# Weighting a one-hot matrix on ScalarE instead of VectorE, in a two-block transformer kernel

## The chip, the cores and the metric

The kernel runs on one core of one Trainium2 chip. The metric is the device time of one execution in microseconds (us). An execution of the kernel before takes 3455.06 us (median of 3 runs, 3452.7 to 3456.17).

## The reference

Two transformer blocks in fp32 over 512 tokens of width 1024: a hybrid of gated delta rule and sparse attention with a gated feed-forward, then a hybrid of two linear-attention mixers with a PEER feed-forward. The change lies in that last one. PEER holds 16384 experts, numbered by pairs of 128 x 128 keys. For each token and each of 8 heads it takes the 16 best pairs with softmax weights:

```
        idx = jnp.take_along_axis(cand_idx.reshape(n, PEER_HEADS, -1), pos, axis=-1)
        w = jax.nn.softmax(best, axis=-1)
        u = jnp.take(u_tab, idx, axis=0)
        act = jax.nn.gelu(jnp.einsum('nhkd,nd->nhk', u, hb).astype(jnp.float32))
        out = jnp.einsum('nhk,nhkd->nd', w * act, jnp.take(v_tab, idx, axis=0))
```

Each token so has 128 chosen experts (i, j) with weights w.

## The kernel before

The program is written engine by engine, with its own semaphores; nothing is reordered by a scheduler. For the first 64 tokens the experts' rows are gathered by GpSimd. For the other 448 the kernel works densely, in two stages:

- **The u stage** multiplies all 16384 experts by the 448 tokens. Each fp32 product is made of three matmuls (high times high, high times low, low times high). `u_pe` has 128 steps t of two halves with 12 matmuls of 128x448 each; two steps share one weight tile of 128x2048, so a tile ends with every odd step. ScalarE (`u_sc`) makes the high part of the tile two ahead as soon as the tile before it in the same buffer is used up (`next_high`, line 516, `wh`), and then a gelu (line 2959, `gst`) after each step. VectorE (`u_ve`) makes the low part (line 523, `wl`). SyncE (`u_sy`) loads tiles (`ring<-in_u`) and spills each gelu to HBM (`gelu_spill<-gst`); there are two `gst` buffers, and a gelu waits until the spill two steps earlier has landed.
- **The v stage** reads the gelus and a dense 128x128 table of weights per token back, multiplies them (`weigh`) and multiplies the result by the v table.

The dense weight tables are built beside the u stage, from the chosen pairs. `choose` does this in four blocks j of 128 tokens: `top` finds the best 16 pairs per head (VectorE mostly), `hot` builds the tables of the block. For a token, two one-hot matrices of 128 pairs by 128 keys are formed on VectorE and multiplied on TensorE: `Bh` says the second key of each pair, `Ah` the first key and carries the pair's weight. `ijw` holds i, j and w of the block with the 128 pairs on the partitions, one column per token. A step of `hot` handles four tokens, called a quad here; there are 112 (16 in block 0, 32 in each of blocks 1 to 3). `Ah` and `Bh` have three buffers each. Per quad:

- `hot_ve`, VectorE: one comparison of 128x512 for `Bh` (line 2895) and four instructions of 128x128 for `Ah` (lines 2897 to 2899), each a comparison and a multiplication by the weight at once; then semaphore `ab`. From the fourth quad on it first waits for the products of three quads earlier (`ab_mm`).
- `hot_pe`, TensorE: waits for `ab`, then four products into one of three PSUM banks (line 2865; the matmuls themselves are issued on line 568), `ab_mm`. Each fp32 product counts as two matmuls in the trace, so a quad shows as x8.
- `hot_sc`, ScalarE: waits for `ab_mm`, then copies the bank into `stage` (line 2879), `stg`. `hot_sy` spills `stage` after every 16 quads (`weight_spill`, four transfers of SyncE).

`weave` fixes the order of each engine's instructions: the steps of the u stage and of `choose` alternate one to 1.05, and within `choose` the steps of `hot(j)` and `top(j + 1)` alternate one to 0.75, the last block's `hot(3)` running alone. `hot_ve` starts its first quad two steps before `hot_pe` does. Every engine executes its own list strictly in this order:

```
    CHOOSE = 1.05
...
        together((u_pe(p), 1), (choose_pe(p), CHOOSE))
...
            yield from weave((hot(j), 1), (top(j + 1), 0.75))
```

Of the kernel before, what the change touches and what calls it, by code (L numbers as in the profile page):

```python
# [7 lines left out]
ALU = mybir.AluOpType  # L8
ACT = mybir.ActivationFunctionType
AX = mybir.AxisListType  # L10
M, A_, S_ = ALU.mult, ALU.add, ALU.subtract
# [140 lines left out]
def bc(ap, n):  # L152
    a = ap.unsqueeze(2)
    return a.to_broadcast([a.shape[0], a.shape[1], n])


def rep(ap, n):
    a = ap.unsqueeze(1)
    return a.to_broadcast([a.shape[0], n, a.shape[2]])


def flat(ap):
    return ap.rearrange("p a b -> p (a b)")


def quad(ap):
    return ap.rearrange("p (a b) -> p a b", a=4)
# [47 lines left out]
def build(nc, D, shapes):  # L215
    with ExitStack() as ctx:
        _build(nc, D, ctx)
# [56 lines left out]
def _build(nc, D, ctx):  # L274
    s = Sems(nc, ctx)
# [3 lines left out]
    def sb(name, shape, dt=F32, c=ctx):  # L279
        return c.enter_context(nc.sbuf_tensor(name, shape, dt))  # L280

    cst = sb("cst", [128, D["consts"].shape[1]])
    C = {k: cst[:, o:o + n] for k, (o, n) in CONST.items()}
# [166 lines left out]
    with ExitStack() as ar:  # L450
# [9 lines left out]
        ijw = sb("ijw", [128, 3, 128], F32, ar)  # L460
        red8 = sb("red8", [128, 2, 8], F32, ar)
        Ah = [sb(f"Ah{j}", [128, 4, 128], F32, ar) for j in range(3)]
# [103 lines left out]
    def mm(p, out, pairs, start=True, stop=True, check=True):  # L566
        for i, (l, r) in enumerate(pairs):
            ins = p.e.matmul(out, l, r, start=start and i == 0, stop=stop and i == len(pairs) - 1,  # L568
                             skip_group_check=not check)
        return ins  # L570
# [7 lines left out]
    def tr(p, out, in_):  # L578
        k = in_.shape[0]
        return p.e.transpose(out, in_, ident[0:k, 0:k])  # L580
# [2261 lines left out]
    def quads(j):  # L2842

        return [(32 * j + q - 16, q) for q in range(16 if j == 0 else 0, 32)]
# [3 lines left out]
    def hot_pe(p, j):  # L2848
        yield
        yield  # L2850
        p.wait_ge(s("wsel"), j + 1)
        if j:
            p.wait_ge(s("ijw"), j)
        for c in range(3):
            ins = tr(p, bank[4][:, 128 * c:128 * c + 128], sel[:, c, :])
        p.then_inc(ins, s("ijw_mm"))
        yield
        yield
        yield
        for t, q in quads(j):  # L2860
            if t >= 3:
                p.wait_ge(s("stg"), t - 2)
            p.wait_ge(s("ab"), t + 1)
            for z in range(4):
                ins = mm(p, bank[5 + t % 3][:, 128 * z:128 * z + 128], [(Ah[t % 3][:, z, :], Bh[t % 3][:, z, :])],
                         start=z == 0, check=False)
            p.then_inc(ins, s("ab_mm"))
            yield
        yield

    def hot_sc(a, j):
        for _ in range(5):
            yield
        for t, q in quads(j):
            b, place = t // 16, stage[t // 16 % 2]
            if b >= 2:
                a.wait_ge(s(f"wst{b % 2}"), 64 * (b // 2))
            a.wait_ge(s("ab_mm"), t + 1)
            a.then_inc(a.e.activation(place[:, :, 4 * (q % 16):4 * (q % 16) + 4].rearrange("p j t -> p t j"),  # L2879
                                      quad(bank[5 + t % 3][:, :]), ACT.Copy), s("stg"))  # L2880
            yield
        yield

    def hot_ve(v, j):
        for _ in range(3):
            yield
        v.wait_ge(s("ijw_mm"), j + 1)
        if j:
            v.wait_ge(s("ab"), 32 * j - 16)
        v.then_inc(v.e.tensor_copy(flat(ijw[:, :, :]), bank[4][:, 0:384]), s("ijw"))  # L2890
        v.settle()
        for t, q in quads(j):
            if t >= 3:
                v.wait_ge(s("ab_mm"), t - 2)
            v.e.tensor_tensor(Bh[t % 3][:, :, :], rep(C["iota"], 4), bc(ijw[:, 1, 4 * q:4 * q + 4], 128), ALU.is_equal)
            for z in range(4):
                k = 4 * q + z
                ins = v.e.tensor_scalar(Ah[t % 3][:, z, :], C["iota"], ijw[:, 0, k:k + 1], ijw[:, 2, k:k + 1],  # L2898
                                        ALU.is_equal, M)
            v.then_inc(ins, s("ab"))  # L2900
            yield
        for _ in range(3):
            yield
# [22 lines left out]
    def choose_pe(p):  # L2926
        yield from choose(lambda j: top_idle(), lambda j: hot_pe(p, j), start_pe(p))

    def choose_sc(a):
        yield from choose(lambda j: top_sc(a, j), lambda j: hot_sc(a, j), start_sc(a))  # L2930

    def choose_ve(v):
        yield from choose(lambda j: top_ve(v, j), lambda j: hot_ve(v, j), start_ve(v))
# [517 lines left out]
```

## Time and profile before

| | |
|---|---|
| median of 3 runs | 3455.06 us |
| the profiled execution | 3454.81 us, of which span of the trace 3453.0 us |
| TensorE matmul (PE) busy | 3302.8 us, 96% |
| TensorE weight load (PEld) busy | 2952.9 us, 86% |
| VectorE (DVE) busy | 2099.1 us, 61% |
| ScalarE (ACT) busy | 1187.8 us, 34% |
| GpSimd (POOL) busy | 178.4 us, 5% |
| mean granted TensorE clock | 0.961 of full speed |

The 0.961 is a mean: at any moment the clock is at one of two levels, full (2.4 GHz) or half (1.2 GHz). The u stage lies between 2050 and 2794 us of the span, the quads between 2147 and 2740 us, the v stage behind. Matmuls overlap, so their busy time says that work was always in the array, not that it ran at its peak; their starts are the better measure. Lines are named by their number in the kernel before.

### The profile page before, as it was taken

Reading aid. Unit: us, or ns where it says so; the run is one execution under the profiler, and the core shown is the slowest. Engines: PE = TensorE matmul, PEld = TensorE weight load, DVE = VectorE, ACT = ScalarE, POOL = GpSimd, SP = SyncE. Lnnn points to the kernel's source line nnn. Section 1 sums busy time; section 2 is a strip of 40 time slices with the busy share of each in tenths; the row PEclk is TensorE's granted clock in tenths of the full one; section 3 lists DMA queues with packets and bytes.
Section 4 is the critical chain, followed back from the end, with each engine's and each line's share of the span. In section 5 each row is a group of like instructions: output and inputs, shape, how many; then the busy total and the mean of one; then the engine's idle time right before and its main releaser. Section 6 shows DMA issues by size and latency. Waiting matters only on the chain.

```text
span 3453.0 us, 43509 instructions
## 1 busy us (share of the span) xinstructions
PE 3302.8 (96%) x18086; PEld 2952.9 (86%) x18086; DVE 2099.1 (61%) x3724; ACT 1187.8 (34%) x1580; POOL 178.4 (5%) x133
## 2 busy tenths in 40 slices
PE   7998989999998899999899998999999999999998
PEld 7887977878788789988778787999999989999997
DVE  5456854747434344666644339998797557677774
ACT  2244232222233333455532222444444422222222
POOL 0000000000000000000000000000000012233330
PEclk9898998999999998999999899999999999999998
DMA  6232111232331133121233243545555689999992
GB/s 233 82 134 98 49 74 55 82 114 78 105 105 55 58 136 107 59 77 62 102 118 147 98 160 130 166 163 174 199 173 181 221 300 320 319 320 315 316 314 81
DMA packets 213332, 525.03 MB, mean 152 GB/s; under 512 B 12272, under 2 KB 143856, under 8 KB 177040
## 3 DMA queue, kind: packets, MB, share of 16 engines
q1 hardware_dynamic: 192512, 447.11, 37.0%
q0 software_dynamic: 18464, 67.15, 5.9%
q10 hardware_dynamic: 2160, 7.99, 0.6%
q8 instruction: 143, 2.34, 0.3%
q14 instruction: 53, 0.43, 0.0%
HBM read 439.33 MB, written 82.84 MB: 151 GB/s over the span
## 4 chain that ended last, share of the span: by engine, by line
PE 84%; DVE 8%; ACT 4%; DMA 2%; issue 1%; SPq 0%; ACTq 0%; DVEq 0%
PE bank L568 75%; PE bank L632 2%; PE bank L1201 2%; DVE wl L523 1%; ACT wh L516 1%; PE bank L2413 1%; PE bank L639 1%; PE bank L580 1%; ACT sgm L2481 1%; DMA wv<-weight_spill 1%; DVE ub L3063 0%; PE bank L1440 0%; PE bank L2422 0%; DMA cst<-in_consts 0%; DVE acc L149 0%
## 5 line engine op out<-in xcount | busy, mean ns | idle before, releaser
L568 PE MATMUL bank<-hh,wh 128*128 128x512 f32 (+2 forms) x2512 | 953.7, 380 | 35.1 <-DVE wl L523 15.8
L568 PE MATMUL bank<-hl,wh 128*128 128x512 f32 (+2 forms) x2512 | 925.6, 368 | 0.0
L568 PE MATMUL bank<-hh,wl 128*128 128x512 f32 (+2 forms) x2512 | 923.8, 368 | 0.0
L523 DVE TENSOR_TENSOR wl<-ring,wh 128x2048 fp32r<-128x2048 f32 (+2 forms) x250 | 557.1, 2229 | 547.6 <-ACT wh L516 547.5
L516 ACT ACTIVATE wh<-ring 128x2048 fp32r<-128x2048 f32 (+2 forms) x250 | 465.6, 1863 | 978.0 <-PE bank L568 968.2
L568 PEld LDWEIGHTS bank<-hh,wh 128*128 128x128 f32 x2512 | 484.6, 193 | 106.4 <-issue 28.2
L568 PEld LDWEIGHTS bank<-hl,wh 128*128 128x128 f32 x2512 | 484.1, 193 | 65.4 <-issue 6.3
L568 PEld LDWEIGHTS bank<-hh,wl 128*128 128x128 f32 x2512 | 483.1, 192 | 62.5
L568 PE MATMUL bank<-ph,wh 128*128 128x448 f32 x1024 | 371.8, 363 | 10.5 <-DVE pl L3028 10.5
L568 PE MATMUL bank<-ph,wl 128*128 128x448 f32 x1024 | 371.7, 363 | 0.0
L568 PE MATMUL bank<-pl,wh 128*128 128x448 f32 x1024 | 371.6, 363 | 0.0
L568 PEld LDWEIGHTS bank<-ph,wh 128*128 128x128 f32 x1024 | 192.3, 188 | 26.8 <-issue 13.6
L568 PEld LDWEIGHTS bank<-pl,wh 128*128 128x128 f32 x1024 | 192.6, 188 | 13.6
L568 PEld LDWEIGHTS bank<-ph,wl 128*128 128x128 f32 x1024 | 192.5, 188 | 11.7
L568 PE MATMUL bank<-wh,hh 128*128 128x256 f32 (+2 forms) x520 | 155.8, 300 | 0.0
L2879 ACT ACTIVATE stage<-bank 128x512 f32<-128x512 f32 x112 | 123.1, 1108 | 91.0 <-PE bank L568 89.9
L568 PE MATMUL bank<-wh,hl 128*128 128x256 f32 (+2 forms) x520 | 151.0, 290 | 0.0
L568 PE MATMUL bank<-wl,hh 128*128 128x256 f32 (+2 forms) x520 | 151.0, 290 | 0.0
L3051 POOL DMA_INDIRECT ub<-in_urow,gsel x64 | 86.8, 1357 | 854.3 <-DMA weight_spill<-stage 566.5
L2898 DVE TENSOR_SCALAR Ah<-cst,ijw 128x128 f32<-128x128 f32 x448 | 124.8, 345 | 0.0
L2959 ACT ACTIVATE gst<-bank 128x448 f32<-128x448 f32 x128 | 68.5, 537 | 159.8 <-PE bank L568 116.9
L568 PEld LDWEIGHTS bank<-Bh,Ah 128*128 128x128 f32 x896 | 117.0, 191 | 3.2 <-issue 0.4
(489 smaller groups left out, 4461.0 us busy)
## 6 DMA issues: line engine op xcount, KB each, us to landing
ring<-in_v SPq DMA_DIRECT2D x68, 1024.0 KB
ring<-in_u SPq DMA_DIRECT2D x64, 1024.0 KB
gelu_spill<-gst SPq DMA_DIRECT2D x128, 224.0 KB, 1.9
weight_spill<-stage SPq DMA_DIRECT2D x28, 1024.0 KB, 9.3
gv<-gelu_spill SPq DMA_DIRECT2D x64, 448.0 KB, 4.7
wv<-weight_spill SPq DMA_DIRECT2D x64, 448.0 KB, 7.4
ring<-in_ada SPq DMA_DIRECT2D x24, 1024.0 KB
ring<-in_wup SPq DMA_DIRECT2D x22, 1024.0 KB
```

Source lines behind the costliest of these rows:

```text
L516: a.then_inc(a.e.activation(wh[q % 2][:, 0:n], ring[k % 4][:, 0:n], ACT.Copy), s("whi"))
L523: v.then_inc(v.e.tensor_tensor(wl[q % 2][:, 0:n], ring[k % 4][:, 0:n], wh[q % 2][:, 0:n].bitcast(F32), S_), s("parts"))
L568: ins = p.e.matmul(out, l, r, start=start and i == 0, stop=stop and i == len(pairs) - 1, skip_group_check=not check)
L580: return p.e.transpose(out, in_, ident[0:k, 0:k])
L632: ins = p.e.matmul(out[:, j:j + 1], sq[:, 128 * j:128 * j + 128], C["ones"][:, 0:1], start=start and j == 0, stop=stop, skip_group_check=True)
L639: ins = p.e.matmul(out[:, 128 * j:128 * j + 128], r[:, j:j + 1].to_broadcast([128, 128]), ident, start=j == 0, stop=True, skip_group_check ...
L1201: ins = p.e.matmul(ps[:, 128 * h:128 * h + 128], l, r, start=h == 0 and n_ == 0, stop=True, skip_group_check=True)
L2413: p.then_inc(p.e.matmul(bank[7][:, :], l, r, start=True, stop=True), s("ss_mm"))
L2879: a.then_inc(a.e.activation(place[:, :, 4 * (q % 16):4 * (q % 16) + 4].rearrange("p j t -> p t j"), quad(bank[5 + t % 3][:, :]), ACT.Copy) ...
L2898: ins = v.e.tensor_scalar(Ah[t % 3][:, z, :], C["iota"], ijw[:, 0, k:k + 1], ijw[:, 2, k:k + 1], ALU.is_equal, M)
L2959: a.then_inc(a.e.activation(gst[t % 2][:, :], bank[t % 4][:, 0:ND], ACT.Gelu_apprx_tanh), s("ge_u"))
L3051: g.e.indirect_dma_start(ub[n % 4][:, :], None, D["urow" if n < 64 else "vrow"], bass.IndirectOffsetOnAxis(gsel[:, 0, n % 64:n % 64 + 1], ...
```

## The change

`Ah` is made in two steps on two engines. VectorE makes one comparison of 128x512 for the four tokens, as for `Bh`, without the weight. A new function `weight_sc` has ScalarE wait for it and multiply each of the four 128x128 pieces in place by its column of weights, and then raise a new semaphore `aw`, which `hot_pe` waits for instead of `ab`. In ScalarE's order the multiplication of a quad stands one step of `hot` ahead of that of TensorE's products: in front of the copy of the quad before.

```diff
         for t, q in quads(j):
             if t >= 3:
                 p.wait_ge(s("stg"), t - 2)
-            p.wait_ge(s("ab"), t + 1)
+            p.wait_ge(s("aw"), t + 1)
...
+    def weight_sc(a, t, q):
+        a.wait_ge(s("ab"), t + 1)
+        for z in range(4):
+            k = 4 * q + z
+            ins = a.e.activation(Ah[t % 3][:, z, :], Ah[t % 3][:, z, :], ACT.Copy, scale=ijw[:, 2, k:k + 1])
+        a.then_inc(ins, s("aw"))
+
     def hot_sc(a, j):
-        for _ in range(5):
-            yield
-        for t, q in quads(j):
+        for _ in range(4):
+            yield
+        weight_sc(a, *quads(j)[0])
+        yield
+        for n, (t, q) in enumerate(quads(j)):
+            if n + 1 < len(quads(j)):
+                weight_sc(a, *quads(j)[n + 1])
             b, place = t // 16, stage[t // 16 % 2]
...
         if j:
-            v.wait_ge(s("ab"), 32 * j - 16)
+            v.wait_ge(s("aw"), 32 * j - 16)
         v.then_inc(v.e.tensor_copy(flat(ijw[:, :, :]), bank[4][:, 0:384]), s("ijw"))
...
             v.e.tensor_tensor(Bh[t % 3][:, :, :], rep(C["iota"], 4), bc(ijw[:, 1, 4 * q:4 * q + 4], 128), ALU.is_equal)
-            for z in range(4):
-                k = 4 * q + z
-                ins = v.e.tensor_scalar(Ah[t % 3][:, z, :], C["iota"], ijw[:, 0, k:k + 1], ijw[:, 2, k:k + 1],
-                                        ALU.is_equal, M)
-            v.then_inc(ins, s("ab"))
+            v.then_inc(v.e.tensor_tensor(Ah[t % 3][:, :, :], rep(C["iota"], 4), bc(ijw[:, 0, 4 * q:4 * q + 4], 128),
+                                         ALU.is_equal), s("ab"))
```

The order of the instructions shows where the new ones stand. First ScalarE at the start of block 3; `sel` is the exponential that ends `top(3)`, `wh` the high part of a tile, `gst` the gelu of a u step, `stage` the copy of a quad. Before:

```order
L2758 ACTIVATE sel<-sel 128x128
L2959 ACT_TABLE_LOAD
L2959 ACTIVATE gst<-bank 128x448
L516 ACTIVATE wh<-ring 128x2048
L2959 ACTIVATE gst<-bank 128x448 x2
L2879 ACTIVATE stage<-bank 128x4x128 x2
L516 ACTIVATE wh<-ring 128x2048
```

and now (the functions behind the edit stand 8 to 11 lines lower):

```order
L2758 ACTIVATE sel<-sel 128x128
L2967 ACT_TABLE_LOAD
L2967 ACTIVATE gst<-bank 128x448
L516 ACTIVATE wh<-ring 128x2048
L2967 ACTIVATE gst<-bank 128x448
L2875 ACTIVATE Ah<-Ah,ijw 128x128 x4
L2967 ACTIVATE gst<-bank 128x448
L2875 ACTIVATE Ah<-Ah,ijw 128x128 x4
L2890 ACTIVATE stage<-bank 128x4x128
L2875 ACTIVATE Ah<-Ah,ijw 128x128 x4
L2890 ACTIVATE stage<-bank 128x4x128
L516 ACTIVATE wh<-ring 128x2048
```

The multiplication of the block's first quad stands between two gelus, that of the second behind the later gelu. Further on in the same block, at the end of a tile, ScalarE's order before is

```order
L516 ACTIVATE wh<-ring 128x2048
L2959 ACTIVATE gst<-bank 128x448
L2879 ACTIVATE stage<-bank 128x4x128 x2
L2959 ACTIVATE gst<-bank 128x448
L2879 ACTIVATE stage<-bank 128x4x128 x2
```

and now

```order
L516 ACTIVATE wh<-ring 128x2048
L2967 ACTIVATE gst<-bank 128x448
L2875 ACTIVATE Ah<-Ah,ijw 128x128 x4
L2890 ACTIVATE stage<-bank 128x4x128
L2875 ACTIVATE Ah<-Ah,ijw 128x128 x4
L2890 ACTIVATE stage<-bank 128x4x128
L2967 ACTIVATE gst<-bank 128x448
```

So at the end of a tile the weights of the next quad now come behind the high part and the gelu. The order on TensorE is the same as before; on VectorE one instruction stands in each place of four; SyncE and GpSimd are as before.

## Rows read from the trace of the kernel before

**Rows 1.** The page, part 1: busy us, share of the span, instructions.

```profile
PE 3302.8 (96%) x18086; PEld 2952.9 (86%) x18086; DVE 2099.1 (61%) x3724; ACT 1187.8 (34%) x1580; POOL 178.4 (5%) x133
```

**Rows 2.** Windows: stretch, its us, busy PE, PEld, DVE, ACT, POOL; PEclk, DMA share, GB/s.

```profile
2250.00:2350.00 100.00, 100.00 (x548) 93.71 (x547) 92.62 (x272) 44.03 (x44) 0.00 (x0) 1.00 0.43 150
```

**Rows 3.** Groups by line, 2145 to 2745 us: busy us, mean ns | idle before, releaser.

```profile
L2898 DVE TENSOR_SCALAR Ah<-cst,ijw 128x128 f32<-128x128 f32 x448 | 124.8, 345 | 0.0
L2879 ACT ACTIVATE stage<-bank 128x512 f32<-128x512 f32 x112 | 123.1, 1108 | 91.0 <-PE bank L568 89.9 <-issue 1.2
...
L516 ACT ACTIVATE wh<-ring 128x2048 fp32r<-128x2048 f32 x51 | 97.8, 1917 | 116.9 <-PE bank L568 115.5 <-issue 1.4
...
L2895 DVE TENSOR_TENSOR Bh<-cst,ijw 128x512 f32<-128x512 f32 x112 | 76.6, 684 | 10.1 <-PE bank L568 8.3 <-issue 1.6
```

**Rows 4.** Waits, 2145 to 2745 us: us in total, times, longest.

```profile
DVE wl L523 <- ACT wh L516: 72.1, 30, 8.3
ACT gst L2959 <- DMA gelu_spill<-gst: 29.3, 6, 8.7
```

**Rows 5.** Timeline (start, us, engine, line, what), PE and ACT, a tile's end.

```profile
2656.28 1.05 PE L568 MATMUL bank<-Bh,Ah 128*128 128x128 f32 x8
...
2656.54 1.92 ACT L516 ACTIVATE wh<-ring 128x2048 fp32r<-128x2048 f32 x1 [1.38 <-PE bank L568]
2658.36 0.53 ACT L2959 ACTIVATE gst<-bank 128x448 f32<-128x448 f32 x1
2658.79 1.12 ACT L2879 ACTIVATE stage<-bank 128x512 f32<-128x512 f32 x1
...
2659.61 1.05 PE L568 MATMUL bank<-Bh,Ah 128*128 128x128 f32 x8
```

**Rows 6.** ACT pieces of 128x128 with an operand per partition: timeline, then groups by form.

```profile
1600.09 2.16 ACT L2481 ACTIVATE sgm<-bank,nac 128x128 f32<-128x128 f32 x8
...
L2481 ACT ACTIVATE sgm<-bank,nac 128x128 f32<-128x128 f32 x128 | 34.7, 390 | 0.0
```

**Rows 7.** Timeline of DVE and PE at the quad that VectorE delivers last.

```profile
2504.65 1.12 DVE L2898 TENSOR_SCALAR Ah<-cst,ijw 128x128 f32<-128x128 f32 x4
2505.68 0.69 DVE L2895 TENSOR_TENSOR Bh<-cst,ijw 128x512 f32<-128x512 f32 x1
...
2506.01 1.05 PE L568 MATMUL bank<-Bh,Ah 128*128 128x128 f32 x8
```

**Rows 8.** Timeline of ACT and PE at three gelus that wait for a spill.

```profile
2461.58 1.05 PE L568 MATMUL bank<-Bh,Ah 128*128 128x128 f32 x8
2461.59 0.53 ACT L2959 ACTIVATE gst<-bank 128x448 f32<-128x448 f32 x1
...
2562.23 1.05 PE L568 MATMUL bank<-Bh,Ah 128*128 128x128 f32 x8
...
2562.45 0.55 ACT L2959 ACTIVATE gst<-bank 128x448 f32<-128x448 f32 x1 [7.08 <-PE bank L568]
...
2639.68 1.05 PE L568 MATMUL bank<-Bh,Ah 128*128 128x128 f32 x8
...
2642.79 0.55 ACT L2959 ACTIVATE gst<-bank 128x448 f32<-128x448 f32 x1 [8.68 <-DMA gelu_spill<-gst]
```

**Rows 9.** Timeline of PE and ACT where two quads follow without u work between.

```profile
2682.84 1.95 PE L568 MATMUL bank<-Bh,Ah 128*128 128x128 f32 x16
...
2684.92 0.53 ACT L2959 ACTIVATE gst<-bank 128x448 f32<-128x448 f32 x1
```

**Rows 10.** Windows around two gaps of TensorE, columns as in rows 2.

```profile
2771.20:2773.50 2.30, 0.02 (x1) 0.02 (x1) 2.23 (x2) 0.54 (x1) 0.00 (x0) 1.00 0.92 376
...
2774.50:2777.90 3.40, 3.40 (x11) 3.00 (x10) 0.24 (x1) 2.62 (x3) 0.00 (x0) 0.50 0.95 345
2777.90:2784.50 6.60, 6.60 (x34) 6.10 (x34) 2.06 (x1) 0.71 (x2) 0.00 (x0) 1.00 0.70 245
...
3168.00:3172.00 4.00, 2.70 (x14) 2.23 (x13) 3.11 (x3) 2.76 (x2) 2.35 (x2) 1.00 0.75 222
```

## The prediction

> **What bounds the kernel now.** I read the page's busy times first: TensorE is busy in 96% of the span, VectorE in 61%, ScalarE in 34% [rows 1]. That is a mean over many stages, so I then cut out the stretch with the quads, by the windows: in 100 us of it TensorE is busy for 100.00 us at the full clock, VectorE for 92.62, ScalarE for 44.03 [rows 2]. VectorE looks crowded, but no row has TensorE idle for it: the groups by line show TensorE work without a gap. So TensorE sets the pace here, VectorE's and ScalarE's work is worth what TensorE waits for, and the question is not how much work is taken off VectorE but how early each quad's `Ah` is ready. Third, the waits: ScalarE's gelu waits for its spill buffer six times, 29.3 us in total and up to 8.7 us at once, and VectorE once waits 8.3 us for a high part that stood behind such a gelu [rows 4]. These waits cost nothing now, since TensorE has four banks for the u steps. Fourth, the timeline at single quads, for who is late by how much.
>
> **Off VectorE.** Per quad, four instructions of 345 ns [rows 3] go. They overlap: from the start of the first to the start of what follows is 2505.68 - 2504.65 = 1.03 us [rows 7]. In their place comes one comparison of the form of `Bh`, 684 ns [rows 3], of which I count 0.62 us until the next can start, by the same overlap. So 0.41 us of VectorE's time is saved per quad, 46 us over 112. Nearly all of it lies beside a TensorE that never waited. The exception is where VectorE is latest: `Ah` ends there at 2504.65 + 1.12 = 2505.77, and the products start at 2506.01, with the load of their first operand some 0.2 us earlier (my estimate, the time of one matmul) [rows 7]. Two quads of the 112 are like this, and TensorE loses about 0.4 us at them together. With the saving of the nine and more quads since VectorE last waited (some 4 us) both are early enough. **Term 1: -0.4 us.**
>
> **Onto ScalarE.** Four multiplications of 128x128 with an operand per partition, 448 in all. The trace has the same form elsewhere: eight in a row take 2.16 us, one of them alone 390 ns [rows 6], so (2.16 - 0.39) / 7 = 0.25 us from start to start. A quad then takes 3 x 0.25 + 0.39 = 1.15 us. Bounds: 1.0 us, four starts of 0.25 with nothing for the last one's end, and 1.56 us if in-place work from SBUF did not overlap at all, 4 x 390 ns. I take 1.15, since that row has eight of them back to back. ScalarE gets 448 x 0.25 = 112 us more in 600 us, 19 in 100, where it is busy for 44 [rows 2]: as a whole it fits.
>
> The Trainium skill ("ScalarE: Activation LUTs", What ACT_TABLE_LOAD costs) gives 186 ns + 0.833 ns per column, 93 ns more for each pointer operand, and an overlap of 93 ns back to back: an estimate of 1.27 us per quad, 0.12 us more than the row says. By it the sum would be some 2 us higher. The chip's row decides here.
>
> **The new wait.** `Ah` now goes VectorE, ScalarE, TensorE. On ScalarE's list the weights of a quad stand behind whatever stood there before: a high part (which starts only when TensorE ends a tile), gelus (which wait for their own u step and for a spill), the weights and copies before. Behind the new wait are queued the copy, the next gelu and high part, and through them VectorE's low part; TensorE waits for the weights themselves. The weights of the next quad can be late in three kinds of place.
>
> (a) *A tile ends, a quad follows, then only 12 matmuls, then the next quad.* The timeline shows one: the quad starts at 2656.28, ScalarE's high part at 2656.54, its gelu at 2658.36, and the engine is free for the next instruction at 2658.79; TensorE starts the next quad at 2659.61, its first load some 0.2 us before, at 2659.41 [rows 5]. The weights would run from 2658.79 to 2659.94, and some 0.05 us later TensorE sees them: late by 2659.99 - 2659.41 = 0.58 us. Each such place is a stall of its own, since ScalarE starts afresh from the end of TensorE's tile. In TensorE's order I count 16 (3, 2, 5 and 6 in blocks 0 to 3); where 24 matmuls follow, there are 12 more at 6.60 / 34 = 0.19 us [rows 10], 2.3 us, and nothing is late. With an even step in place of a tile's end there is no high part in front and about 1.2 us is left. **Term 2: 16 x 0.58 = 9.3 us**; 6.9 with a quad of 1.0 us, 15.8 with one of 1.56.
>
> (b) *A gelu held by its spill stands in front.* The timeline has three that matter [rows 8]. The gelu at 2642.79 was held for 8.68 us; the engine is free 0.44 us later, the weights of the block's second quad are ready at 2643.23 + 1.20 = 2644.43, and TensorE wants them at 2639.68 - 0.2: 4.95 us. The gelu at 2562.45 (its 7.08 us are put down to PE, but its u step was long over): ready at 2562.89 + 1.20 = 2564.09, wanted at 2562.03: 2.06 us. At 2461.59 a gelu ends a row of a held gelu, a high part and itself: ready at 2462.02 + 1.20 = 2463.22, wanted at 2461.38: 1.84 us. The remaining held gelus are early enough or late by a quarter of a microsecond; I add 0.4 for two of them. **Term 3: 9.3 us.** What makes these spills late is SyncE's list, with a spill of weights or a load in front; the change leaves it alone, so I leave the waits as they are.
>
> (c) *Two quads without u work between.* Once in block 3, right at a tile's end: the pair's 16 matmuls start at 2682.84 and run 1.95 us, so the second quad starts about 1.0 us in and its load at 2683.65, while ScalarE is free at 2684.92 + 0.43 = 2685.35 [rows 9] and ready at 2686.55. **Term 4: 2.9 us.**
>
> **The clock.** A gap of 2.30 us before u matmuls is followed by 3.40 us at a clock of 0.50, in which 11 matmuls run; behind it 34 run in 6.60 us [rows 10], so 17.5 would have run in 3.40, and the 6.5 that are missing take 1.3 us. The gap of some 1.3 us at 3168 leaves the clock at 1.00 [rows 10]. So the stalls of 0.58 us should cost no clock, those of 4.95 and 2.9 us some, and those of 2.06 and 1.84 us lie between the two rows. I take three. **Term 5: 3 x 1.3 = 4 us**, 0 to 7.
>
> **The sum.** -0.4 + 9.3 + 9.3 + 2.9 + 4 = +25. After the quads TensorE goes on with the u stage and the v stage, busy all through; everything they need (spills, gathers, weights) is shifted with the last quads, so I see nothing that takes the delay back, nor any that adds. The profiled execution took 3454.81 us, 0.25 us below the median of the runs shown, so the sum goes onto the median: 3455 + 25 = 3480 us.
>
> **The rivals.**
> *ScalarE becomes the chain (larger).* If the held gelus reach TensorE in full, because the weights of the quads around them have no lead left, terms 3 and 4 grow from 12 to the 29.3 us of rows 4 and the 7.1 us of the one put down to PE, 36 us; with the longer quad (term 2 at 15.8) the sum is -0.4 + 15.8 + 36 + 6 = +57, with the likely one +51. For it: a spill that is late now meets a ScalarE with less idle time. Against it: the idle time in front of the copies and high parts is 91 and 117 us [rows 3], and a quad behind 24 matmuls has 2.3 us in hand. About 3508 us.
> *The held gelus dissolve (smaller).* TensorE's new pauses give the spills time, and the three places of term 3 shrink to kind (a). Then -0.4 + 9.3 + 1.7 + 2.9 + 1.3 = +15: 3470 us. For it: SyncE's list has only a fixed amount of work. Against it: the pauses come one step at a time and shift SyncE's triggers with them.
> *Not slower.* VectorE is the engine that is really late, and the weights are ready in time at every tile's end. The place is kind (a), and it decides at one number: the quad's weights must take under 0.57 us from 2658.79. Then terms 2 to 5 nearly vanish and 3455 - 0.4 stays; for more than that to be won, TensorE would have to wait for VectorE at more than the two quads found. VectorE's 92.62 us of 100 speak for it; that four instructions of at least 0.25 us each do not fit into 0.57 us speaks against. 3455 us.
> That the change doesn't do what it says is ruled out by the order: the new multiplications stand where the text puts them.
>
> **How the numbers follow.** The forecast 0.70, the larger rival 0.12, the smaller 0.10, not slower 0.08. About 0.2% (7 us) is what a measurement of this kernel can tell from no change. The first three are slower by more than that, save for the smallest corner of the smaller one; the last is mostly the same. That gives slower 0.90, same 0.07, faster 0.03. The forecast's own bounds: 3455 + 14 (short quad, no clock term, half of term 3) to 3455 + 36 (long quad at all 21 places, full clock). The range reaches to the smaller rival's lower part, 3466, and towards the larger, 3504.
>
> **What would show it.** Right: VectorE's group of `Ah` is x112 at about 685 ns; ScalarE has 448 new instructions of about 390 ns; in the waits, TensorE's products of a quad wait for ScalarE's `Ah` some 20 times, 21 us in all, most of them 0.6 us at a tile's end and the longest, near 5 us, at the second quad of block 3; behind the long ones the clock falls to half; VectorE's idle time grows by about 70 us. Wrong: waits at quads behind 24 matmuls (the chain is ScalarE's), no waits at tile ends (the instruction is much cheaper than its like), or a time taken back in the v stage.

## The result and the profile after

The changed kernel takes 3473.4 us (median of 4 runs, 3469.96 to 3475.93), the kernel before beside it 3453.88 us (4 runs, 3450.49 to 3456.17): a ratio of 1.0057 with a 95% interval of 1.0039 to 1.0074, or 19.5 us slower (13 to 26). The forecast was +25 us, 3480, with a range of 3466 to 3504. So it held, a few microseconds too high; the sections below go through the terms one by one. Every run, of this kernel and of those below, was a fast one.

| | before | after |
|---|---|---|
| profiled span | 3453.0 us | 3471.6 us |
| VectorE busy | 2099.1 us | 2053.1 us |
| ScalarE busy | 1187.8 us | 1308.1 us |
| first quad to start of the v stage | 643.7 us | 667.5 us |

The last line is from the load for the first quad's products to the first matmul of the v stage, in the two traces. It leaves out what differs by chance ahead of it: the work there is the same in both programs, and yet the first quad starts 4.7 us earlier in the trace of after (in the ten traces of this document it starts between 2145.4 and 2155.5 us). 23.8 us are lost inside, 4.7 of them hidden in the comparison of the two spans. It is still one trace of each kernel. Up to the last quad 25.4 us are lost; the 56.3 us behind it are 1.6 us shorter than before, and `before_gst3` below shows that this is not time made up. The rest of the program, from the start of the v stage on, takes 657.9 us (658.4 before).

The page of after, part 1 and four groups of part 5 (against rows 1 and 3):

```profile
PE 3303.8 (95%) x18086; PEld 2948.6 (85%) x18086; DVE 2053.1 (59%) x3388; ACT 1308.1 (38%) x2028; POOL 180.8 (5%) x133
...
L523 DVE TENSOR_TENSOR wl<-ring,wh 128x2048 fp32r<-128x2048 f32 (+2 forms) x250 | 557.1, 2229 | 591.1 <-ACT wh L516 591.1
...
L2875 ACT ACTIVATE Ah<-Ah,ijw 128x128 f32<-128x128 f32 x448 | 141.3, 390 | 1.4 <-DVE Ah L2907 1.3
...
L568 PE MATMUL bank<-Bh,Ah 128*128 128x128 f32 x896 | 120.7, 278 | 17.3 <-ACT Ah L2875 17.3
...
L2890 ACT ACTIVATE stage<-bank 128x512 f32<-128x512 f32 x112 | 121.7, 1087 | 30.6 <-PE bank L568 30.5
```

VectorE's busy time fell by 46.0 us, as worked out (0.41 x 112 = 46), and none of it came back in time. The new instruction on ScalarE takes 390 ns, like its model in [rows 6]. What is new is the idle time of TensorE in front of a quad's products, 17.3 us, put down to ScalarE's `Ah`. VectorE's wait for the high part grew from 547.6 us on the page before to 591.1: it has more spare time and spends it waiting. Two stretches, to be set against [rows 2]:

```profile
2250.00:2350.00 100.00, 99.57 (x548) 92.89 (x547) 86.57 (x224) 61.97 (x109) 0.00 (x0) 1.00 0.41 147
...
2550.00:2650.00 100.00, 93.33 (x517) 86.47 (x516) 64.19 (x114) 58.68 (x103) 0.00 (x0) 0.98 0.60 200
```

ScalarE went from 44 to 62 of 100 us, VectorE from 93 to 87, and TensorE is no longer at 100.

The waits between 2140 and 2770 us (us in total, times, longest), against [rows 4]:

```profile
DVE wl L523 <- ACT wh L516: 117.2, 42, 9.3
...
ACT gst L2967 <- DMA gelu_spill<-gst: 30.3, 6, 8.7
PEld bank L568 <- issue: 24.4, 22, 5.3
PE bank L568 <- ACT Ah L2875: 17.3, 20, 5.0
...
ACT Ah L2875 <- DVE Ah L2907: 1.3, 2, 1.1
```

The row PE <- ACT Ah did not exist before: 20 times, up to 5.0 us (the row PEld <- issue is the same standstill, seen at the weight loads). ScalarE hardly ever waits for VectorE's comparison (1.3 us), so the chain's first link is in time, and its second is late. ScalarE's waits for spills are what they were.

**A tile's end**, the kind of place that was counted 16 times (timeline of after, ScalarE and TensorE; compare [rows 5]):

```profile
2668.96 1.05 PE L568 MATMUL bank<-Bh,Ah 128*128 128x128 f32 x8
...
2669.22 1.91 ACT L516 ACTIVATE wh<-ring 128x2048 fp32r<-128x2048 f32 x1 [1.38 <-PE bank L568]
2671.04 0.52 ACT L2967 ACTIVATE gst<-bank 128x448 f32<-128x448 f32 x1
2671.46 1.27 ACT L2875 ACTIVATE Ah<-Ah,ijw 128x128 f32<-128x128 f32 x4
...
2672.87 1.13 PE L568 MATMUL bank<-Bh,Ah 128*128 128x128 f32 x8 [0.44 <-ACT Ah L2875]
```

High part, gelu, weights stand in a row on ScalarE; the next quad of TensorE starts with the end of the weights. It was 3.33 us behind its neighbour in [rows 5] and is 3.91 us behind here. The idle time printed is 0.44 us, less than the delay, because a matmul's end is modelled as overlapping the next start; measured at the loads the delay from quad to quad is 0.75 us, of which 0.09 us returns at the quad after. By the starts of the matmuls it is 0.58 us here and 0.08 us more at the next quad, so 0.66 us stay either way. The matmuls start 0.14 us after the end of the weights (2671.46 + 1.27 = 2672.73, then 2672.87).

**The held gelu at the second quad of block 3** (against the last pair of [rows 8]; then the window behind it):

```profile
2647.86 0.54 ACT L2967 ACTIVATE gst<-bank 128x448 f32<-128x448 f32 x1 [7.68 <-DMA gelu_spill<-gst]
2648.30 1.26 ACT L2875 ACTIVATE Ah<-Ah,ijw 128x128 f32<-128x128 f32 x4
...
2649.70 2.05 PE L568 MATMUL bank<-Bh,Ah 128*128 128x128 f32 x8 [4.96 <-ACT Ah L2875]
```

```profile
2647.10:2653.90 6.80, 4.20 (x15) 3.97 (x16) 1.29 (x2) 4.73 (x11) 0.00 (x0) 0.51 0.43 179
```

TensorE stands still for 4.96 us, then runs the quad in 2.05 us instead of 1.05: the granted clock is at half in this stretch (0.51 in the mean of the window).

### The profile page after: what moved, and what is told of

Read it like the earlier page. It is cut to its first block, busy times and chain, and to the rows that moved or that the text cites. A ratio compares the mean times of both kernels' runs of the same rounds, so it can differ in the third digit from the quotient of the medians.

```text
span 3471.6 us, 43623 instructions
## 1 busy us (share of the span) xinstructions
PE 3303.8 (95%) x18086; PEld 2948.6 (85%) x18086; DVE 2053.1 (59%) x3388; ACT 1308.1 (38%) x2028; POOL 180.8 (5%) x133
## 3 DMA queue, kind: packets, MB, share of 16 engines
q8 instruction: 143, 2.34, 0.3%
## 4 chain that ended last, share of the span: by engine, by line
PE 80%; DVE 8%; ACT 6%; DMA 2%; issue 2%; SPq 1%; ACTq 0%; DVEq 0%
PE bank L568 72%; PE bank L632 2%; PE bank L1201 2%; ACT wh L516 2%; DVE wl L523 1%; SPq L2922 1%; PE bank L2413 1%; PE bank L639 1%; PE bank L580 1%; ACT Ah L2875 1%; ACT sgm L2481 1%; DMA gelu_spill<-gst 1%; DMA wv<-weight_spill 1%; DVE ub L3071 0%; PE bank L1440 0%
## 5 line engine op out<-in xcount | busy, mean ns | idle before, releaser
L523 DVE TENSOR_TENSOR wl<-ring,wh 128x2048 fp32r<-128x2048 f32 (+2 forms) x250 | 557.1, 2229 | 591.1 <-ACT wh L516 591.1
L2875 ACT ACTIVATE Ah<-Ah,ijw 128x128 f32<-128x128 f32 x448 | 141.3, 390 | 1.4 <-DVE Ah L2907 1.3
L568 PE MATMUL bank<-Bh,Ah 128*128 128x128 f32 x896 | 120.7, 278 | 17.3 <-ACT Ah L2875 17.3
```

Of the source, the lines that this page charges most:

```text
L523: v.then_inc(v.e.tensor_tensor(wl[q % 2][:, 0:n], ring[k % 4][:, 0:n], wh[q % 2][:, 0:n].bitcast(F32), S_), s("parts"))
L2875: ins = a.e.activation(Ah[t % 3][:, z, :], Ah[t % 3][:, z, :], ACT.Copy, scale=ijw[:, 2, k:k + 1])
```

## The experiments

Each was measured beside runs of the kernel before on the same chip. "Stage" is the length defined above; 643.7 us before, 667.5 after. "Late at quad n" is by how much the distance from quad n - 1 to quad n grew against the kernel before, from the traces; quads are numbered 0 to 111 over the four blocks, and their distance is taken at the load of the first product. The first four experiments stood beside a kernel before of 3453.9 us, the last four beside one of 3451.7. The ratio is an estimate over the fast runs and not the quotient of the two medians: for `lead2` it says 3 us, the medians stand 5.1 us apart.

| run | time, us | ratio, 95% interval | stage, us |
|---|---|---|---|
| changed kernel | 3473.4 | 1.0057, 1.0039 to 1.0074 | 667.5 |
| act_only | 3474.5 | 1.0062, 1.0045 to 1.0078 | 666.3 |
| ve_only | 3450.8 | 0.9993, 0.9984 to 1.0003 | 641.5 |
| half | 3464.0 | 1.0032, 1.0019 to 1.0044 | 654.4 |
| lead2 | 3459.0 | 1.0009, 1.0000 to 1.0019 | 648.1 |
| before_gst3 | 3452.0 | 0.9996, 0.9986 to 1.0005 | 641.2 |
| after_gst3 | 3466.5 | 1.0048, 1.0031 to 1.0064 | 657.1 |
| lead2_gst3 | 3451.5 | 1.0005, 0.9996 to 1.0015 | 641.9 |
| pool_w | 3454.6 | 1.0009, 0.9999 to 1.0018 | 644.0 |

### One half of the change each

`act_only` keeps the four weighted comparisons on VectorE and adds ScalarE's pass with a factor of one:

```diff
-            ins = a.e.activation(Ah[t % 3][:, z, :], Ah[t % 3][:, z, :], ACT.Copy, scale=ijw[:, 2, k:k + 1])
+            ins = a.e.activation(Ah[t % 3][:, z, :], Ah[t % 3][:, z, :], ACT.Copy, scale=C["ones"][:, 0:1])
```

> VectorE makes Ah as in the kernel before, weight included; ScalarE passes over it in the changed kernel's places, multiplying by a column of ones. Theory (the loss is the position of ScalarE's step in its list): the same stalls as in the changed kernel at the same quads, 16 of 0.75 us, 2.1 at quad 48, 5 at quad 81, 3 at quad 95, so at least +24 us on the before; a little more, up to +30, since VectorE is 0.41 us slower per quad and late around quads 57 to 61. Rival (the one comparison of 128x512 on VectorE, or its traffic, costs something): clearly under +20.

It has the whole loss: 1.0062, 20.6 us between the medians, 22.6 us in the stage and 24.8 up to the last quad. Medians and stage are under the "at least +24" that I had expected. The same quads are late by the same amounts, 0.75 us at the tile ends, 1.93 at quad 48, 5.13 at quad 81, 3.10 at quad 95. The waits between 2140 and 2770 us:

```profile
PE bank L568 <- ACT Ah L2875: 16.6, 20, 4.8
...
ACT Ah L2875 <- DVE Ah L2909: 11.3, 9, 2.3
```

TensorE's wait for ScalarE is as in the changed kernel. The second row is the one place where VectorE's saving shows: without it ScalarE waits 11.3 us for VectorE instead of 1.3. TensorE does not feel it; the extra I had expected for the quads around 57 to 61 did not come. Quad 61 is even 0.37 us earlier than in the kernel before, with the four weighted comparisons on VectorE as they were: TensorE is 1.93 us late from quad 48 on, and VectorE has that time.

`ve_only` is the kernel before with the one comparison, and leaves the weights of the pairs out:

```diff
-            for z in range(4):
-                k = 4 * q + z
-                ins = v.e.tensor_scalar(Ah[t % 3][:, z, :], C["iota"], ijw[:, 0, k:k + 1], ijw[:, 2, k:k + 1],
-                                        ALU.is_equal, M)
-            v.then_inc(ins, s("ab"))
+            v.then_inc(v.e.tensor_tensor(Ah[t % 3][:, :, :], rep(C["iota"], 4), bc(ijw[:, 0, 4 * q:4 * q + 4], 128),
+                                         ALU.is_equal), s("ab"))
```

> Only the VectorE half: one comparison per quad, TensorE waits for VectorE as before, the weights of the pairs are left out. Theory: no stall of TensorE at any quad, -0.4 us at quads 57 and 61, total within 2 us of the before. Rival (the comparison costs): slower than the before by over 5 us. A third view, that VectorE was what bounded the stage: faster by over 7 us.

No quad is late and one is earlier, quad 61 by 0.37 us. Here it is VectorE's saving: from the start of a quad's `Bh` to TensorE's load of that quad, 1.83 us pass at quad 61 in the kernel before and 6.40 here. The saving is not the only way to it, as `act_only` showed and `before_gst3` shows below. Its groups between 2140 and 2745 us:

```profile
L523 DVE TENSOR_TENSOR wl<-ring,wh 128x2048 fp32r<-128x2048 f32 x52 | 119.1, 2290 | 108.2 <-ACT wh L516 108.2
...
L2896 DVE TENSOR_TENSOR Ah<-cst,ijw 128x512 f32<-128x512 f32 x112 | 76.8, 686 | 0.0
```

VectorE does `Ah` in 76.8 us instead of 124.8 [rows 3] and waits 108.2 us for high parts, where it waited 72.1 [rows 4]: the saving turns into waiting. The time, 0.9993 (0.9984 to 1.0003), can't be told from no change. The stage is 2.2 us shorter, and 1.9 of them lie behind the last quad, where no comparison is left to be faster (see `before_gst3`). The two runs together put the whole loss on ScalarE's half.

### Half of ScalarE's work

```diff
     def weight_sc(a, t, q):
         a.wait_ge(s("ab"), t + 1)
-        for z in range(4):
+        for z in range(2):
```

Two of each quad's four tokens go without their weights.

> As the changed kernel, but only two of a quad's four pieces are multiplied on ScalarE; the other two tokens go without their weights. Theory (a stall is the time by which the pieces end after TensorE's turn): each place shrinks by the 0.58 us of two pieces: the 16 tile ends from 0.75 to some 0.15 to 0.2 us, quad 81 from 5.3 to 4.7, quad 95 from 3.1 to 2.5, quad 48 from 2.1 to 1.5; total some +13 us on the before with the clock. Rival (ScalarE's sum of work): half of the loss, +10, spread over all places alike, also the held ones: quad 81 at 2.6.

The tile ends went from 0.75 to 0.17 us, quad 81 from 5.29 to 4.60, quad 95 from 3.10 to 2.51, quad 48 from 2.08 to 1.28. A quad of two pieces takes 0.69 us here where four took 1.27:

```profile
2663.55 1.91 ACT L516 ACTIVATE wh<-ring 128x2048 fp32r<-128x2048 f32 x1 [1.38 <-PE bank L568]
2665.37 0.53 ACT L2967 ACTIVATE gst<-bank 128x448 f32<-128x448 f32 x1
2665.80 0.69 ACT L2875 ACTIVATE Ah<-Ah,ijw 128x128 f32<-128x128 f32 x2
```

So the stalls at tile ends shrink by 0.58 us, the length taken away, and not to a half; a long one stays long. That is the mark of a place that comes too late, not of an engine with too much work. The total alone would not have decided it: 10.1 us between the medians (7 to 15 by the interval) is as near to the rival's +10 as to my +13. Up to the last quad the delay is 13.2 us.

### The same work, placed earlier

`lead2` does a quad's weights two steps ahead of its products, behind the copy, and the first two quads of a block together:

```diff
-        weight_sc(a, *quads(j)[0])
+        for x in range(2):
+            weight_sc(a, *quads(j)[x])
         yield
         for n, (t, q) in enumerate(quads(j)):
-            if n + 1 < len(quads(j)):
-                weight_sc(a, *quads(j)[n + 1])
...
                                       quad(bank[5 + t % 3][:, :]), ACT.Copy), s("stg"))
+            if n + 2 < len(quads(j)):
+                weight_sc(a, *quads(j)[n + 2])
             yield
```

> As the changed kernel, but ScalarE multiplies a quad two steps ahead of TensorE's products and behind the copy, instead of one step ahead and in front of it; the work is the same. Theory (position): the stalls at the 16 tile ends, at quads 68, 81 and 95 are gone, the one of some 2 us at quad 48 stays; total within 4 us of the before. Rival (ScalarE has too much work, or the chain over three engines is too long): at least half of the loss stays, over +10 us.

All 16 tile ends, quads 68, 81 and 95 are on time, with the same 448 instructions on ScalarE; 1.0009 (1.0000 to 1.0019), 5.1 us between the medians and 4.4 in the stage, so at the edge of the 4 us expected. ScalarE now waits 29.0 us for VectorE's comparisons (27 times), without harm to a quad. Quad 48 is late by 2.12 us as expected. What I had missed is quad 82, late by 2.67 us, and a stretch at half clock behind it (1.47 us at quad 83); quads 16 and 96 are late by 0.44 and 0.74 us:

```profile
2649.16 0.54 ACT L2968 ACTIVATE gst<-bank 128x448 f32<-128x448 f32 x1 [4.34 <-DMA gelu_spill<-gst]
2649.60 1.02 ACT L2889 ACTIVATE stage<-bank 128x512 f32<-128x512 f32 x1
2650.41 1.24 ACT L2875 ACTIVATE Ah<-Ah,ijw 128x128 f32<-128x128 f32 x4
...
2651.79 1.13 PE L568 MATMUL bank<-Bh,Ah 128*128 128x128 f32 x8 [2.34 <-ACT Ah L2875]
```

The held gelu that stood in front of quad 81's weights now stands in front of quad 82's. A greater lead moves the victim and shortens its stall; it does not take the hold away.

### The hold taken away

The three `_gst3` runs give the gelus a third buffer, which has no room of its own and lies on constants that are read for the last time in the first block:

```diff
         gst = [sb(f"gst{j}", [128, ND], F32, ar) for j in range(2)]
+        gst.append(cst[:, CONST["lvl0"][0]:CONST["lvl0"][0] + ND])
...
-            if t >= 2:
-                a.wait_ge(s(f"gst{t % 2}"), 16 * (t // 2))
-            a.then_inc(a.e.activation(gst[t % 2][:, :], bank[t % 4][:, 0:ND], ACT.Gelu_apprx_tanh), s("ge_u"))
+            if t >= 3:
+                a.wait_ge(s(f"gst{t % 3}"), 16 * (t // 3))
+            a.then_inc(a.e.activation(gst[t % 3][:, :], bank[t % 4][:, 0:ND], ACT.Gelu_apprx_tanh), s("ge_u"))
...
```

SyncE's spills, and its waits for them before the v stage, are changed to the three buffers in the same way.

> The changed kernel with the third gelu buffer. Theory (held gelus are a part of their own): the stalls at quads 48, 68 (beyond its neighbour at a tile's end), 81 and the half clock behind them go, some 10 us; the 16 tile ends of 0.75 us and the pair at 95 with its clock, 16 to 17 us, stay; with the 4 us won as in the before with three buffers the total is +12 to +13 us on the before. Rival (a long ScalarE list is late anyway): the stall at quad 81 stays over 2 us and the total at +17 or more.

The stalls at quads 48, 68 and 81 are gone, as is the clock behind quad 81. The tile ends (0.75, but 1.03 at quad 15) and the pair (3.10 us at quad 95, 1.58 at quad 96) are as before this edit. TensorE's wait went from 17.3 us to this:

```profile
PE bank L569 <- ACT Ah L2876: 10.1, 17, 2.9
```

The stage is 10.4 us shorter than the changed kernel's. The total, 1.0048 (1.0031 to 1.0064) or +17 us (14.8 between the medians), is above the +12 to +13 that I had expected but holds it in its interval. By the total alone the rival's "+17 or more" would not be ruled out; it is by quad 81, which is on time. Against the before with three buffers the stage is 15.9 us longer.

> The kernel before with a third buffer for the gelus (in a piece of the constants that is no longer read), so that ScalarE waits for the spill of three steps ago, not two. Theory: ScalarE's waits for spills shrink from 30 us to a few; before the v stage the gap of 2.3 us, which came from a high part behind a held gelu, and the half clock behind it go, -3 to -4 us; nothing else, since no quad hung on a held gelu. Rival (held gelus never cost TensorE anything): within 1 us of the before.

The quads of the kernel before do not move (only quad 61, 0.37 us earlier). The stage is 2.5 us shorter, but 0.9996 (0.9986 to 1.0005) is no measurable gain, and the -3 to -4 us that I expected can't be confirmed. Nor is the shorter stage the third buffer's doing. The gap in front of the v stage is still there, 1.65 us for 2.28; what is gone is the stretch at half clock behind it [rows 10]. The gap, then the 3.4 us from a microsecond behind it (columns as in rows 2):

```profile
2775.46:2777.11 1.65, 0.00 (x1) 0.00 (x1) 1.59 (x1) 1.16 (x2) 0.00 (x0) 1.00 0.97 405
2778.10:2781.50 3.40, 3.40 (x19) 3.15 (x18) 2.29 (x1) 0.73 (x2) 0.00 (x0) 1.00 1.03 419
```

`ve_only`, with two gelu buffers, shows the same:

```profile
2767.84:2769.78 1.94, 0.00 (x2) 0.01 (x1) 1.88 (x1) 0.54 (x1) 0.00 (x0) 1.00 0.96 393
2770.80:2774.20 3.40, 3.40 (x19) 3.15 (x18) 0.22 (x1) 2.60 (x3) 0.00 (x0) 1.00 0.86 314
```

In all ten traces TensorE waits there for a low part, 1.3 to 2.9 us. Only in the kernel before and in `pool_w` (2.28 and 2.88 us) does half clock follow, and only there do 57.9 and 58.5 us pass from the last quad to the v stage; in the other eight it is 55.4 to 56.3. So some 2 us of each stage that is compared with the kernel before stand for this one place.

> Both cures: weights two steps ahead, three gelu buffers. Theory: no quad is late by more than half a microsecond, and the total is that of the kernel before with three gelu buffers within 2 us, so some 3 us under the before. Rival (the work on ScalarE costs by itself): at least 4 us above the before with three buffers.

With both cures no quad is late, save 0.73 us at quad 96, and the stage is 641.9 us, 0.7 us over `before_gst3`. The time is 1.0005 (0.9996 to 1.0015) of the before. So the 448 instructions on ScalarE cost nothing by themselves that could be measured. It doesn't beat the before either, where I had expected some 3 us: what VectorE's saving has to win is the 0.37 us of quad 61, and `before_gst3` has them without it.

### Another third engine

`pool_w` leaves ScalarE's list as it was and puts the weights on GpSimd, which is idle in this stage, as one instruction per quad:

```diff
+        for j in range(4):
+            for t, q in quads(j):
+                g.wait_ge(s("ab"), t + 1)
+                g.then_inc(g.e.tensor_tensor(Ah[t % 3][:, :, :], Ah[t % 3][:, :, :],
+                                             bc(ijw[:, 2, 4 * q:4 * q + 4], 128), M), s("aw"))
```

> VectorE as in the changed kernel, but GpSimd, idle in this stage, multiplies each quad by its weights in one instruction of 128x512; ScalarE's list is that of the kernel before. Theory (the place in ScalarE's list costs, not the third engine in the chain): no stalls at tile ends nor behind held gelus, if a quad takes GpSimd under some 2 us; total within 3 us of the before. Rival (a chain over three engines is too long, or GpSimd slows VectorE): stalls at many quads, over +10 us.

No quad is late, stage 644.0 us, 1.0009 (0.9999 to 1.0018), 2.9 us between the medians. The stage is 2.5 us longer than that of `ve_only`, all of it behind the last quad. A chain over three engines does no harm where the middle engine has nothing in front of the work. Two groups between 2140 and 2745 us:

```profile
L3047 POOL TENSOR_TENSOR Ah<-Ah,ijw 128x512 f32<-128x512 f32 x112 | 149.2, 1332 | 443.8 <-DVE Ah L2896 443.8
...
L2896 DVE TENSOR_TENSOR Ah<-cst,ijw 128x512 f32<-128x512 f32 x112 | 103.6, 925 | 0.0
```

## Why the prediction was right, by its steps

| term | forecast, us | measured in the trace, us |
|---|---|---|
| 1: VectorE late at two quads | -0.4 | -0.4 (quad 61), see below |
| 2: 16 tile ends | 9.3 | 12.2, of which 1.3 given back |
| 3: held gelus | 9.3 | 8.5 (quads 16, 48, 68, 81) |
| 4: the pair at quad 95 | 2.9 | 3.1 |
| 5: half clock | 4 | 3.4 |
| behind the last quad | 0 | -1.6, see below |
| sum | 25 | 23.8 (before rounding) |

- **What bounds.** Right. VectorE at 92.62 of 100 us was not what anything hung on; `ve_only` shows that 46 us less of it gives nothing that can be measured.
- **Off VectorE.** Right to the microsecond in work: one comparison is 685 ns and saves 0.41 us. Term 1 has the right size, and `ve_only` shows that the saving brings it; but in the changed kernel it is not the saving's alone. VectorE is late at quad 61 because it waited near quad 49 for a high part behind a held gelu (the 8.3 us of [rows 4]), and `act_only` (TensorE 1.93 us late there) and `before_gst3` (the hold gone) have the same 0.37 us with VectorE's old work: 4.71 and 4.23 us from the start of `Bh` to TensorE's load at quad 61, for 1.83 before and 6.87 after. Quad 57 had 0.06 us to give, and became a tile end of the new kind.
- **Term 2.** Right in place and count: quads 3, 8, 15, 24, 36, 52, 57, 64, 69, 76, 83, 87, 91, 100, 104, 108 and no others of that kind. The size was off: 0.75 us, not 0.58, or 0.66 with what the next quad gives back. The step that failed is the length of a quad of weights, 1.15 us by the row of `sgm`; it is 1.27 us. By the Trainium skill ("ScalarE: Activation LUTs", What ACT_TABLE_LOAD costs) the estimate had been 4 x 386 - 3 x 93 ns = 1.26 us (the prediction has it as 1.27), and the trace of after agrees. I had taken the trace's row over the page, but that row read from PSUM with an operand for the bias, and the new one works in SBUF with one for the scale; the nearest row was not the same case. Start to start it is 0.29 us, for 0.25 in that row. The rest is the handover: TensorE's load starts 0.11 us after the weights end, and I had counted 0.05.
- **Term 3.** The sum is right, by luck in one part: quad 68 was late by 0.94 us, not 2.06, quad 81 by 5.29, not 4.95, quad 48 by 2.08, not 1.84. The time of a spill moves from one execution to the next (quad 68: 0.52 in `act_only`). `after_gst3` shows that these stalls are the hold's.
- **Term 4.** Right, 3.1 for 2.9.
- **Term 5.** Two stretches at half clock, not three: behind the 5 us and behind the 3 us. The stall at quad 48 (2.1 us late, 1.75 of idle time printed), which I had placed between a row that lost the clock and one that did not, left it full. The other runs narrow it: idle times of 2.27 us (`half`, quad 95) and 2.34 us (`lead2`, quad 82) were followed by half clock, 1.80 us (`lead2`, quad 48) was not; but 2.24 us in front of the v stage in the trace of after was not either, where 2.28 us was in that of before. The first of the two stretches cost more than the 1.3 us of its model (1.8 us, its stretch being twice as long), the second 1.6.
- **Behind the quads.** I had seen nothing there, and named time taken back in the v stage as a sign of being wrong. From the last quad to the v stage 56.3 us pass for 57.9, so 1.6 us less. It is not the delay that is made up: `ve_only`, with no quad late, has 56.0. The trace of before has a stretch at half clock there that eight of the other nine lack. The v stage gives back 0.5 us at most.
- **The total.** The times say 19.5 us with 13 to 26; the stage in the trace says 23.8, and act_only, a second execution of the same loss, 22.6. The forecast of 25 lies in the interval, near its top.
- **The rivals.** ScalarE as the chain is ruled out by the places in `half`, where a long stall stays long, and by `lead2_gst3`, where the same work costs nothing; that the held gelus dissolve, by the 30.3 us of waits for spills that are still there and quad 81 at 5.29 us; that nothing is late, by the times. Of the signs, TensorE waits 20 times as forecast, 17.3 us for 21, and VectorE's idle time grew by 65 us for some 70.

## What to carry to other kernels

Ask of moved work what stands in front of it in the receiving engine's list, not how busy that engine is: ScalarE at 44% lost 24 us of TensorE's time because the weights stood behind a high part, a gelu and at times a held spill, and the same instructions one step earlier and behind the copy cost about a fifth of that (4.4 us of the stage). Work taken off an engine that nobody waits for, even one at 93% busy, was worth nothing that could be measured. And when a wait so far harmless (a gelu on its spill) gets a consumer queued behind it, price it in full at that place.

## What the runs showed of the hardware that was not expected

VectorE and GpSimd make each other wait. In `pool_w` the same comparison of 128x512 takes 925 ns on average instead of 686: 80 of the 112 take 0.67 to 0.69 us, and the 32 that start while GpSimd is at work take 1.52 to 1.53 us (timeline of VectorE and GpSimd):

```profile
2648.65 0.68 DVE L2895 TENSOR_TENSOR Bh<-cst,ijw 128x512 f32<-128x512 f32 x1
2648.81 1.42 POOL L3047 TENSOR_TENSOR Ah<-Ah,ijw 128x512 f32<-128x512 f32 x1 [0.62 <-DVE Ah L2896]
2649.25 1.52 DVE L2896 TENSOR_TENSOR Ah<-cst,ijw 128x512 f32<-128x512 f32 x1
...
2477.81 2.29 DVE L523 TENSOR_TENSOR wl<-ring,wh 128x2048 fp32r<-128x2048 f32 x1
2477.97 3.02 POOL L3047 TENSOR_TENSOR Ah<-Ah,ijw 128x512 f32<-128x512 f32 x1 [3.56 <-DVE Ah L2896]
```

Where the two don't meet, GpSimd's instruction takes 1.04 us. The rows fit turns, not shared speed: the one that starts second does its work when the first has ended. GpSimd, started 0.16 us behind a low part of 2.29 us on VectorE, takes 3.02 us, which is the 2.1 left of that and about its own 1.04, while the low part keeps its length. It is not every instruction of VectorE: 35 of GpSimd's that met only the searches of `top` (MAX8, FIND_INDEX8, MATCH_REPLACE8) took 1.04 us as well. What the two share was not tried. VectorE is busy for 2090.2 us, 38 more than in `ve_only`, 27 of them in `Ah`. No quad is late for it.
